# Moving the last input tiles of the LRU's second group, and the first group's output tiles, in one shared order

## The reference, cut to what matters

```python
xc, new_buf = causal_conv(x_lru, conv_buf, conv_w, conv_b)          # 4 taps along time
r = sigmoid(xb @ w_a + b_a);  i = sigmoid(xb @ w_x + b_x)           # block-diagonal, 16 blocks of 80
log_a = -LRU_C * r * softplus(-lam);  a = exp(log_a)
u = sqrt(-expm1(2.0 * log_a)) * (i * xf)
h[t] = a[t] * h[t-1] + u[t]                                         # a scan along time
lru_branch = (gelu(y_lru) * h) @ w_lru_out
```

## Time and profile before

| | |
|---|---|
| median of 3 runs | 2493.9 us (2491.56 to 2494.48) |
| the profiled execution | 2494.29 us |
| its span | 2492.5 us |
| PE busy | 2435.0 us (98%) |
| POOL busy | 1631.8 us (65%) |
| DVE busy | 1178.5 us (47%) |
| ACT busy | 645.7 us (26%) |
| granted TensorE clock, mean | 0.996 of full |

### The profile page before, as it was taken

How to read it: one execution, slowest core, us unless ns; L and a number is a source line. 1 busy time by engine, 2 the same in 40 slices (tenths; PEclk the granted TensorE clock), 3 DMA queues, 4 the chain that set the end, 5 groups by cost and what they waited for, 6 DMA issues and landing times.

```text
span 2492.5 us, 53934 instructions
## 1 busy us (share of the span) xinstructions
PE 2435.0 (98%) x19636; PEld 2363.4 (95%) x19636; DVE 1178.5 (47%) x1587; ACT 645.7 (26%) x981; POOL 1631.8 (65%) x1685
## 2 busy tenths in 40 slices
PE   7999999999999999999999999999999999999997
PEld 7899989899999999999998999899999999999997
DVE  6645454669744532122247363636786445211223
ACT  2404040446721211011114040404566112100111
POOL 5464646478887766776754555555778777767764
PEclk9999999999999999999999999999999999999998
DMA  6546463522232222322246373635222332323222
GB/s 205 195 149 222 138 225 127 202 87 86 87 102 91 96 89 82 103 93 83 89 163 237 112 248 111 241 120 200 90 78 92 100 93 94 93 80 100 91 83 87
DMA packets 121748, 315.69 MB, mean 127 GB/s; under 512 B 12192, under 2 KB 12960, under 8 KB 121568
## 3 DMA queue, kind: packets, MB, share of 16 engines
q1 hardware_dynamic: 60480, 199.78, 25.5%
q10 hardware_dynamic: 61088, 113.34, 12.8%
HBM read 272.69 MB, written 40.38 MB: 126 GB/s over the span
## 4 chain that ended last, share of the span: by engine, by line
PE 79%; DVE 8%; DVEq 4%; DMA 3%; issue 3%; ACT 3%; ACTq 1%; POOLq 0%; POOL 0%
PE proj L363 48%; PE aux L363 26%; DVE scratch L1088 1%; PE aux L566 1%; PE aux L540 1%; DMA out_ret_s<-scratch 1%; PE aux L615 1%; DVE scratch L998 1%; DMA v_rows<-scratch 1%; DVE split_scratch L977 1%; DMA scratch<-in_sret 1%; DVEq L1091 1%; DVE scratch L1146 1%; ACTq L1348 1%; DVEq L1006 0%
## 5 line engine op out<-in xcount | busy, mean ns | idle before, releaser
L351 POOL TENSOR_TENSOR w_low<-w_raw,w_high 128x512 fp32r<-128x512 f32 x840 | 1085.9, 1293 | 124.5 <-issue 1.8
L349 POOL TENSOR_SCALAR w_high<-w_raw 128x512 fp32r<-128x512 f32 x840 | 552.3, 658 | 711.9 <-PE proj L363 545.7
L363 PE MATMUL proj<-x_high,w_high 128*128 128x260 f32 x2752 | 560.5, 285 | 30.7 <-DVE x_low L761 13.7
L363 PE MATMUL proj<-x_high,w_low 128*128 128x260 f32 x2752 | 555.7, 284 | 0.0
L363 PE MATMUL proj<-x_low,w_high 128*128 128x260 f32 x2752 | 555.1, 283 | 0.0
L363 PEld LDWEIGHTS proj<-x_high,w_high 128*128 128x128 f32 x2752 | 425.9, 189 | 41.8 <-issue 20.8
L363 PEld LDWEIGHTS proj<-x_high,w_low 128*128 128x128 f32 x2752 | 425.6, 189 | 0.0
L363 PEld LDWEIGHTS proj<-x_low,w_high 128*128 128x128 f32 x2752 | 425.1, 189 | 0.0
L363 PE MATMUL proj<-split_scratch,w_high 128*128 128x260 f32 x2544 | 409.2, 283 | 0.0
L363 PEld LDWEIGHTS proj<-split_scratch,w_high 128*128 128x128 f32 x2544 | 348.6, 188 | 5.0 <-issue 5.0
L363 PE MATMUL aux<-x_high,w_high 128*128 128x260 f32 x1344 | 270.8, 283 | 0.0
(11 more groups left out here) (184 smaller groups left out, 2291.0 us busy)
## 6 DMA issues: line engine op xcount, KB each, us to landing
w_raw<-in_wstream SPq DMA_DIRECT2D x252, 512.0 KB, 3.5
scratch<-in_sret ACTq DMA_DIRECT2D x96, 512.0 KB, 7.0
out_ret_s<-scratch ACTq DMA_DIRECT2D x64, 512.0 KB, 3.8
w_raw<-in_wstream SPq DMA_DIRECT2D x72, 448.0 KB, 3.2
w_raw<-in_wstream SPq DMA_DIRECT2D x48, 384.0 KB, 3.0
scratch<-v_rows ACTq DMA_DIRECT2D x64, 256.0 KB, 4.0
w_raw<-in_wstream SPq DMA_DIRECT2D x48, 320.0 KB, 2.8
out_ret_p<-scratch ACTq DMA_DIRECT2D x8, 512.0 KB, 3.0
```

The source lines that it names most:

```text
L349: pool.tensor_scalar(WH[:, j, w], WR[:, j, w], 1.0, 0.0, ALU.mult, ALU.add)
L351: pool.tensor_tensor(WL[:, j, w], WR[:, j, w], WH[:, j, w].bitcast(F32), ALU.subtract).then_inc(s["w_split"], 1)
L363: m = pe.matmul(out, wt[:, w, blk * P:(blk + 1) * P], x[xi], start=first and n == 0, stop=last and n == 2)
```

## The change

Every engine takes its order from one list for both groups. The x tiles (1,3) and (1,4) no longer stand between the groups: x(1,3) comes behind y(1,0) and x(1,4) behind y(1,1). The eight output tiles, which stood 2, 1, 1, 2, 2 behind the five gates of the second group, now stand 0, 0, 2, 3, 3. DVE reads the first two of a gate's output tiles ahead of the scan and a third one behind it. No instruction is added or removed.

```diff
-FILL_X = [(0, 3), (0, 4), (1, 0), (1, 1), (1, 2)]
-FILL_O = [(0, 1), (2,), (3,), (4, 5), (6, 7)]
+FILL_X = [[(0, 3), (0, 4), (1, 0), (1, 1), (1, 2)], [(1, 3), (1, 4)]]
+FILL_O = [(), (), (0, 1), (2, 3, 4), (5, 6, 7)]
...
+for g in range(GROUPS):
+    for t in range(GT):
+        LRU_ORDER += [("y", g, t)] + [("x",) + x for x in FILL_X[g][t:t + 1]]
+        LRU_ORDER += [("o", 0, m) for m in FILL_O[t] if g]
...
+                        if waiting:
+                            conv_low(*waiting)
+                        else:
+                            gated_low(g, t - 1)
+                        gate_input(g, t)
+                        read_y(g, t)
+                        one_less_a2(g, t)
+                        waiting = FILL_X[g][t] if t < len(FILL_X[g]) else None
+                        if waiting:
+                            read_x(*waiting)
+                        filled = FILL_O[t] if g else ()
+                        for m_ in filled[:2]:
+                            read_out(m_)
+                        scan(g, t)
+                        for m_ in filled[2:]:
+                            read_out(m_)
+                        if waiting:
+                            conv(*waiting)
+                            gated_low(g, t)
```

More of the change, by code:

```diff
@@ L685, in _ @@
                 x_tile(0, 2)
[L686 to L694, removed]
+                for g in range(GROUPS):
+                    for t in range(GT):
+                        gates(g, t)
+                        if t < len(FILL_X[g]):
+                            x_tile(*FILL_X[g][t])
+                        if g:
+                            for m_ in FILL_O[t]:
+                                lru_out(m_)
                 with pe.Fori(0, MT // 4) as i:
@@ L1166, in _ @@
                 conv(0, 2)
[L1167 to L1192, removed]
+                waiting = (0, 2)
+                for g in range(GROUPS):
+                    for t in range(GT):
+                        if waiting:
[17 more added lines that the diff above has]
+                            gated_low(g, t)
                 gated_low(1, GT - 1)
@@ L1522, in _ @@
                 first_tap(0, 2)
[L1523 to L1539, removed]
+                waiting = (0, 2)
+                for g in range(GROUPS):
+                    for t in range(GT):
+                        gate_sigmoids(g, t)
+                        if waiting:
+                            conv_high(*waiting)
+                        else:
+                            gated_high(g, t - 1)
+                        gate_decay(g, t)
+                        waiting = FILL_X[g][t] if t < len(FILL_X[g]) else None
+                        if waiting:
+                            first_tap(*waiting)
+                            gated_high(g, t)
                 gated_high(1, GT - 1)
```

## The result

Before: 2492.38 us median of 20 runs (2488.48 to 2498.34). After: 2498.88 us median of 20 (2494.72 to 2504.33). The ratio is 1.0025, with a 95% interval of 1.0018 to 1.0031: the change makes the kernel slower by 4.5 to 7.7 us. Single executions of one kernel differ by up to 10 us, so only medians over many runs tell these orders apart, and the profiles are used for their waits, not for their total time.

The account below looks back on a forecast made before the run. PE, busy for 98% of the span, was taken as the bound. Waits of 5.5 us against 2.85 gave +2.7 a layer, +5.5 in both, one clock fall kept: 2493.9 + 5.5 = 2499.4 us, range 2495.3 to 2504.5.

Parts of the forecast that it names:

- y(1,0): 3.1 us: At y(1,0), PE arrives at 604.02 and waits 3.1 us for `conv_low` of (1,1), which ends at 607.16.
- Nothing that is moved lies ahead: Ahead of `conv_low` of (1,1), DVE and ACT have no moved work, so the 3.1 us wait is read, not guessed.
- Turns of 16.33 us: DVE's turns between `conv_low` of (1,1), (1,2) and (1,3) take 16.33 us each, with POOL at work.
- Sum of the waits: From x(1,2) to y(1,2), PE waits 5.5 to 5.6 us against 2.85 before: +2.7 us a layer.
- the sign that the first layer would end its stage 2.7 us later: In the profile after, the merge would start 2.7 us later than before in the first layer.
- The clock as a fixed sum: Behind PE's waits, one fall to the lower clock, costing 2.63 us, is carried over at no change in cost.
- Moving the output tiles back is worth nothing: In the second group, moving the output tiles gains nothing, as no wait stood there before.
- More is lost: Rival: DVE turns of 17 to 19 us, y(1,3) waiting too, or two more clock falls: +8 to +12 us; chance 0.18.
- Faster: Rival: the second group starts earlier and the 2.85 us waits go with nothing in their place: 2488.2 us; chance 0.06.
- The rival with the clock up: Rival: waits as computed but no clock fall, +2.9 us, 2496.8; shares chance 0.29 with short turns.
- exclusive lock: DVE and GpSimd contend for a shared port pair by a lock, so the contended turn of 16.33 us holds, not 15.27.
- The clock rule: The array's clock halves when its monitor sees an idle window; shorter waits would meet it less often: +2.9 instead of +5.5.

Follow-up runs that it names:

- e5: The changed kernel with GpSimd's second instruction of each split cut to 16 columns and `w_low` zeroed at the start: 2471.23 us, one execution.
- e4: The changed kernel with 16 added matmuls ahead of the `conv_low` waits of y(1,0) and y(1,1): 2499.78 us against 2495.11 for the kernel before, ratio 1.0017.
- e2: The kernel before with only the output tiles moved (0, 0, 2, 3, 3): 2496.34 us against 2495.11 for the kernel before, ratio 1.0007.
- e1: The changed kernel with output tiles back at 2, 1, 1, 2, 2, only x tiles moved: 2492.25 us against 2495.11 for the kernel before, ratio 0.9993.
- e3: The changed kernel with output tiles spread 1, 1, 1, 2, 3: 2494.59 us against 2495.11 for the kernel before, ratio 0.9997.
- e8: The kernel before with only DVE's read of x(1,3) moved ahead of the scan of (0,4): 2494.81 us against 2494.83, ratio 1.0002.
- e7: The kernel before with x(1,4) moved behind y(1,0) and x(1,3) read ahead of the scan of (0,4): 2489.16 us against 2494.83, ratio 0.9978.
- e6: The kernel before with GpSimd's second instruction of each split cut to 16 columns and `w_low` zeroed at the start: 2471.49 us, one execution.

## Why the prediction was right, point by point

The forecast was +5.5 us; the interval is +4.5 to +7.7 (the ratio times 2492.38). Direction, place and cause of the waits held. Two terms were off, in opposite directions, and one idea about the clock was incomplete; that the sum came out this near is in part luck.

- *One wait goes, waits for `conv_low` come at y(1,0), y(1,1), y(1,2).* Shown by the profile after, line by line.
- *y(1,0): 3.1 us.* It was 2.08 and 2.06. PE left x(1,2) at 603.2, but `conv_low` of (1,1) ended at 605.15, not 607.16. Of these 2.0 us 0.8 is no gain, as the whole stage ran that much earlier in this profile; the other 1.2 is. "Nothing that is moved lies ahead" overlooked GpSimd: its splits for y(1,0) come there in place of those for x(1,3), and DVE's speed hangs on GpSimd's work (e5). Before, GpSimd (POOL) split 512 columns at a time there without a pause, and DVE's three taps took 3.89 us:

```profile
604.04 1.54 POOL L351 TENSOR_TENSOR w_low<-w_raw,w_high 128x512 fp32r<-128x512 f32 x1
```

After, it has a shorter split and a pause, while PE waits, and the taps took 3.12 us:

```profile
599.54 3.12 DVE L1086 SCALAR_TENSOR_TENSOR scratch<-scratch,params_cur 128x509 f32<-128x509 f32 x3
...
600.12 0.98 POOL L350 TENSOR_TENSOR w_low<-w_raw,w_high 128x256 fp32r<-128x256 f32 x1
...
605.86 0.41 POOL L348 TENSOR_SCALAR w_high<-w_raw 128x256 fp32r<-128x256 f32 x1 [2.06 <-PE proj L362]
```

That these splits made that one turn shorter is argued from the rows, not shown by an experiment.
- *Turns of 16.33 us.* This is the term that was too small. In the changed kernel they were 17.38 and 17.07 us from end to end of `conv_low`; in e4, where the clock stays up, PE resumes 17.26 and 17.38 us apart (607.35, 624.61 and 641.99). I had taken the shortest of three contended turns of the earlier trace rows; their mean, 17.46, was the better guess. I had also hoped for GpSimd's pauses to shorten them; the turns stayed above 17 us in spite of them.
- *Sum of the waits.* From the end of x(1,2) to y(1,2) the prediction had 35.8 us, e4 has 641.99 - 605.09 = 36.9 without a fall of the clock, and the changed kernel's second layer 36.8. Against 42 blocks and the old wait, 33.1, that is +3.8 us a layer and not +2.7. So the sign that the first layer would end its stage 2.7 us later was off as well: it was 4.97, of which the clock (below) explains 1.4.
- *The clock as a fixed sum.* I carried one fall of 2.63 us over at full price. In the first layer of the changed kernel y(1,2) starts without a wait of its own:

```profile
641.36 0.63 PE L362 MATMUL proj<-split_scratch,w_high 128*128 128x260 f32 x4
```

That is 38.3 us behind the end of x(1,2) (603.05; its last pair of matmuls started at 602.81, and pairs follow each other at 0.24 us), 1.4 more than in e4, and the lower clock accounts for them. In the second layer the clock fell too and the distance is 36.8, as in e4: the fall cost nothing there. Before, a fall came behind the last wait of the stage, with nothing to hide it, and its 2.63 us were lost in full. So in these profiles the old order had the dearer fall, and that took back part of the extra 1.1 us a layer. It is one profile of each kernel; how often each order has a fall in these places was not counted.
- *"Moving the output tiles back is worth nothing."* True by itself within the measurement (e2; its waits grew by 0.7 and 1.5 us), wrong as a statement on this change: without an output tile behind y(1,0) and y(1,1) the moved x tiles leave PE too little work, and with them (e1, e3) the loss is gone. My walk had them in no term, though that PE's turns are only 14.4 and 15.9 us long is just their absence.
- *Rivals.* "More is lost" had the right turns (over 17 us), but not the wait at y(1,3), which never came. "Faster" never was near: as long as y(1,0) stands right behind x(1,2), a wait of 2.1 us stays ahead of it, even in e1. The rival with the clock up gave +2.9; e4 has it up in its profile and is at 1.0008 to 1.0026, +2.0 to +6.5, so that rival's price is not excluded; its condition, a clock that stays up in the changed kernel itself, was not met in the one profile.
- *The page of the Trainium skill on the exclusive lock* ("Trainium Architecture — The Big Picture", "What this means for kernel authors"): e5 agrees, 1600 to 1225 ns for a scan when GpSimd's instruction is short; that it is a lock, and not a shared bandwidth, no run here shows. The clock rule ("TensorE: Matmul & The Clock Gate", "What's actually happening"): with idle times broken up, e4's stretches show a granted clock of 1.00. That shorter waits meet a fall less often was not borne out by the one profile after: it has a fall behind waits of 2.70 and 2.06 us.

## What to carry to other kernels

When a list of work is shared by a fast engine and a slower chain of others, write down the fast engine's work between two points at which it needs the chain, and the chain's time for the same stretch. Filler (work that needs nothing from the chain) belongs where the fast engine's work falls furthest short of the chain's time. It counts only together with what else stands there: moving either of two kinds of filler cost nothing measurable here, and moving both cost some 6 us. A wait that goes after one early read may come back at the next resource (e8); what helped (e7) was to give the chain's long turns more of PE's work to hide behind.

## What the runs showed of the hardware that was not expected

- A lower TensorE clock can be free. Behind the waits at 619.96 us (2.70 us) and 1838.41 us (2.06 us) PE ran at the lower level; in the second of them y(1,2) started no later than in e4 with the full clock (36.8 against 36.9 us).
- A fall can follow an idle time of 2.06 us and be missing behind one of 2.85 us (first layer, and the earlier trace rows) or of 2.08 us (605.28 us after).
- Halving GpSimd's work on the splits (1631.8 to 789.5 us busy in the old order), which PE never waits for in the stage in either order, made the whole kernel some 23 us shorter in one execution of each order (2471.23 and 2471.49 against 2494.83). Most of that is idle time of PE: span less busy time was 57.5 us before and is 39.7 in e6.
